# Weight pieces put off only beside attentions, and the modulation units spread thinner over two mixers

## The reference

```
# block 1, two layers: i = 0 is mixer A (grouped-query attention), i = 1 is mixer B (neighbourhood attention)
mod_x = silu(c) @ w_mod[i] + b_mod[i];  mod_c = silu(c_ctx) @ w_mod[i] + b_mod[i]
sh, sc, g = split(mod, 3)                                # shift, scale, gain, 1024 each
hx = rms_norm(x, norm_g[i]) * (1 + sc_x) + sh_x          # the same for the context, hc
yx, yc = mixer(hx, hc, ...)                              # q, k, v, z = h @ w_in; (attention * silu(z)) @ w_out
x = x + g_x * yx;  ctx = ctx + g_c * yc                  # the context only after layer 0
# block 2, one layer
p = _rmsnorm(x) @ w_in_2                                 # m_q, m_k, ..., n_q, ..., n_z, g_a, g_b
ya = sigmoid(m_o) * layernorm(mlstm(silu(conv(m_q)), silu(conv(m_k)), m_v, ...)) * silu(m_z)
yb = nsa(n_q, ...) * silu(n_z)                           # three attentions: compressed, selected, window
merged = sigmoid(g_a) * (ya @ w_branch_a) + sigmoid(g_b) * (yb @ w_branch_b)
out = _rmsnorm(x + merged @ w_out)
```

## Time and profile before

| | |
|---|---|
| three runs | 1679.43, 1682.07, 1684.57 us |
| profiled execution, its own time | 1678.06 us |
| its span | 1676.3 us |
| mean granted clock of PE over the span | 0.969 |
| PE busy | 1570.1 us, 94% |
| DVE, POOL, ACT busy | 725.5, 655.0, 621.6 us |
| weight loads by SP | 98 of 1024 KB |

### The profile page before, as it was taken

One profiled execution on the slowest core, in us unless ns is written; L12 is line 12 of the kernel. 1 busy time (PEld: TensorE's weight loads), 2 busy tenths in 40 slices (PEclk: granted clock), 3 DMA queues, 4 the chain that ended last, 5 costly groups with the idle time before them and its releaser, 6 DMA issues.

```text
span 1676.3 us, 25013 instructions
## 1 busy us (share of the span) xinstructions
PE 1570.1 (94%) x9858; PEld 1225.3 (73%) x9858; DVE 725.5 (43%) x1707; ACT 621.6 (37%) x1301; POOL 655.0 (39%) x640
## 2 busy tenths in 40 slices
PE   5998999999899899999999889999999899998987
PEld 3776777666688788787967677887877765555755
DVE  4334444444542524544465453452415444554023
ACT  4244443434542433334344343443332433332221
POOL 2534443334442533434344353534436243333242
PEclk8999999999999899999999899999999999999998
DMA  9111202221013222222221222212221212111121
GB/s 388 51 51 51 73 29 76 76 76 52 26 55 122 101 70 81 77 76 83 76 70 51 82 79 73 83 69 76 75 76 51 101 51 76 51 51 33 69 85 66
DMA packets 22148, 128.20 MB, mean 76 GB/s; under 512 B 2448, under 2 KB 2576, under 8 KB 8080
## 3 DMA queue, kind: packets, MB, share of 16 engines
q1 hardware_dynamic: 21888, 126.35, 20.8%
q10 hardware_dynamic: 144, 0.26, 0.1%
HBM read 124.50 MB, written 2.10 MB: 76 GB/s over the span
## 4 chain that ended last, share of the span: by engine, by line
PE 80%; DVE 8%; ACT 3%; issue 3%; POOL 3%; DMA 2%; SPq 0%; POOLq 0%; DVEq 0%; ACTq 0%
PE PS L1405 15%; PE PS L1407 14%; PE PS L1406 14%; PE PS L1485 6%; PE PS L1495 6%; PE PS L1520 6%; PE PS L1651 3%; PE PS L1400 2%; PE PS L1401 2%; PE PS L1402 2%; DVE sm L2099 2%; PE PS L1661 2%; POOL WL L2420 2%; DMA W<-in_wu 1%; PE PS L1573 1%
## 5 line engine op out<-in xcount | busy, mean ns | idle before, releaser
L2420 POOL TENSOR_TENSOR WL<-W,WH 128x512 fp32r<-128x512 f32 x280 | 365.2, 1321 | 330.4 <-ACT WH L1681 330.3
L1405 PE MATMUL PS<-HX,WH 128*128 128x512 f32 x1008 | 424.4, 421 | 33.3 <-POOL WL L2420 15.7
L1407 PE MATMUL PS<-HX,WL 128*128 128x512 f32 x1008 | 403.3, 400 | 0.0
L1406 PE MATMUL PS<-LX,WH 128*128 128x512 f32 x1008 | 402.6, 399 | 0.0
L1405 PEld LDWEIGHTS PS<-HX,WH 128*128 128x128 f32 x1008 | 195.3, 194 | 84.3 <-issue 32.2
L1407 PEld LDWEIGHTS PS<-HX,WL 128*128 128x128 f32 x1008 | 194.7, 193 | 43.6
L1406 PEld LDWEIGHTS PS<-LX,WH 128*128 128x128 f32 x1008 | 195.6, 194 | 38.1 <-issue 3.4
L1681 ACT CAST WH<-W 128x512 fp32r<-128x512 f32 x296 | 170.8, 616 | 26.6 <-PE PS L1402 18.5
L1767 ACT ACTIVATE AR<-PS,sm 128x768 f32<-128x768 f32 (+4 forms) x160 | 115.7, 723 | 170.6 <-DVE sm L2104 103.7
L2099 DVE TENSOR_REDUCE sm<-PS 128x1 f32<-128x512 f32 (+4 forms) x224 | 150.1, 670 | 57.8 <-PE PS L1485 53.0
L2487 POOL TENSOR_SCALAR AR<-AR,sm 128x768 f32<-128x768 f32 (+1 forms) x96 | 76.2, 793 | 210.4 <-DVE sm L2115 210.2
(11 more groups left out here) (273 smaller groups left out, 2464.5 us busy)
## 6 DMA issues: line engine op xcount, KB each, us to landing
W<-in_wu SPq DMA_DIRECT2D x98, 1024.0 KB, 4.8
AR<-in_wu SPq DMA_DIRECT2D x8, 1024.0 KB, 11.6
AR<-in_biasb SPq DMA_DIRECT2D x32, 256.0 KB, 2.6
XX<-in_xt SPq DMA_DIRECT2D x2, 1024.0 KB, 6.0
out<-XX SPq DMA_DIRECT2D x8, 256.0 KB, 2.2
XC<-in_xt SPq DMA_DIRECT2D x1, 1024.0 KB, 14.3
C<-in_cc SPq DMA_DIRECT2D x1, 770.5 KB, 8.4
CS<-in_cs SPq DMA_DIRECT2D x1, 512.0 KB, 9.9
```

Of the source, the lines that this page charges most:

```text
L1405: e.matmul(o, wh, xh, start=(k == 0), stop=False)
L1406: e.matmul(o, wh, xl, start=False, stop=False)
L1407: t = e.matmul(o, wl, xh, start=False, stop=(k == 7))
L2420: e.tensor_tensor(WL[:, d, a:z], W[:, n % 2, a:z], WH[:, d, a:z].bitcast(F32), ALU.subtract).then_inc(*s_wl_pool.by(n, q))
```

## The change

It has four parts. Pieces are put off by the rule of 9 only while `attention()` runs (`careful`); elsewhere each tick puts one in. In mixer A each pair from 1 to 7 has one modulation unit, in the first half of its queries, and pair 7 a second one in the last half of its gates; `aout` has four, as before, and the last four of the list go into the second half of each `bz` unit of mixer B. The `gain` steps of layer 1 stand behind `aout`, not ahead of it. In the `wa` units the ticks stand at k = 3 and k = 7 of each half.

```diff
--- before.py
+++ after.py
@@ unit_order
     for i in range(1, 8):
-        u += [("aqz", i)] + (m[2 * i - 2:2 * i] if i < 7 else [])
+        u += [("aqz", i), m[i - 1]]
+    u += [m[7]]
     for i in range(4):
-        u += [("aout", i), m[12 + i]]
+        u += [("aout", i), m[8 + i]]
     for a in range(4):
-        u += [("bz", a - 2)] if a >= 2 else []
+        u += [("bz", a - 2), m[10 + a]] if a >= 2 else []
         u += [("bqk", 2 * a), ("bqk", 2 * a + 1), ("bv", a)]
-    u += [("bz", 2), ("bz", 3)]
+    u += [("bz", 2), m[14], ("bz", 3), m[15]]
@@ tick
-            if pieces and (forced or done_work[0] - loaded_at[pieces[0][0]] > 9):
+            if pieces and (forced or not careful[0] or done_work[0] - loaded_at[pieces[0][0]] > 9):
@@ attention
             spent = [0.0]
+            careful[0] = True
...
             run(fill)
+            careful[0] = False
@@ mixer A
-        units_, riding = iter(MA[:12]), [iter(())]
+        units_, riding = iter(MA[:8]), [iter(())]
...
-                yield from query_group(pair, 0, FX, {1: ride_mm, 5: ride_tr})
+                yield from query_group(pair, 0, FX, {2: ride_mm, 6: ride_tr})
...
-                yield from gate_group(pair, 1, FC, {5: ride_mm_x})
+                yield from gate_group(pair, 1, FC, {3: ride_mm_x, 6: ride_tr} if pair == 7 else {})
                 yield PAUSE
-                ride_tr()
@@ out_proj
-                        run(mod_)
+                        next(mod_, None)
@@ mixer A to B
-        for k in range(0, KC, 2):
-            do("gain", 1, k)
-        out_proj("aout", 0, FULL, False, "o", ["b"], MA[12:])
+        out_proj("aout", 0, FULL, False, "o", ["b"], MA[8:12])
         ar = Arena()
         hb1 = Rows(ar(4096), ar(2048))
+        for k in range(0, KC, 2):
+            do("gain", 1, k)
@@ gen_z
-                yield from pj(("bz", m), un, 0, T, 128 * (m % 2), "b", o)
+                for k in range(8):
+                    yield from pj(("bz", m), un, 0, T, 128 * (m % 2), "b", o, (k,))
+                    if m % 2 and k == 2:
+                        mod_ = mod_units(*MA[12 + a][:1], MA[12 + a][1:], pr)
+                        next(mod_)
+                    if m % 2 and k == 6:
+                        next(mod_)
@@ the wa units
                 for m in range(2):
-                    tick()
                     wps["wa", j, m] = (un.n, bank(FC.take(("wa", j, m), (s_mg, (j, m)))))
                     for k in range(8):
+                        if k % 4 == 3:
+                            tick()
                         do("x_wa", j, m, k)
```

More of the change, by code:

```diff
@@ L294, in build @@
         COST = {"proj": 0.6, "score": 1.0, "turn": 0.5, "pv": 0.7, "x_wa": 0.9, "mod_mm": 0.9, "m_qk": 0.9, "m_num": 1.0}
-        done_work, loaded_at = [0.0], {}
+        done_work, loaded_at, careful = [0.0], {}, [False]
         def do(*item):
@@ L881, in build @@
         norm("b", Arena(6144), X_CTX, [(s_post, ("a", 47))], lambda k, p: [(s_res, ("aout", k, p))])
+        out_proj("aout", 0, FULL, False, "o", ["b"], MA[8:12])
+        ar = Arena()
+        hb1 = Rows(ar(4096), ar(2048))
         for k in range(0, KC, 2):
             do("gain", 1, k)
-        out_proj("aout", 0, FULL, False, "o", ["b"], MA[12:])
-        ar = Arena()
-        hb1 = Rows(ar(4096), ar(2048))
         for part in range(2):
```

## The result

| | before | after |
|---|---|---|
| runs, median | 1682.39 us (4 runs, 1679.43 to 1684.57) | 1642.43 us (4 runs, 1640.18 to 1646.11) |
| profiled execution, its own time | 1678.06 us | 1641.75 us |
| span | 1676.3 us | 1640.0 us |
| mean granted clock | 0.969 | 0.978 |

The ratio is 0.9766, with a 95% interval from 0.9742 to 0.979: 40.0 us less, where 29 were forecast.

The account below looks back on a forecast made before the run. PE, busy 94% of the span, bounds the kernel, so only its idle or slow places can gain. 23.8 + 12.3 − 6.3 − 0.5 = 29.3 us less gives 1653 us in runs, forecast 1648 to 1657, range 1641 to 1668.

Parts of the forecast that it names:

- the clock: Slow stretches behind waits that go: 1.7 us each in mixer A and gb 1, 2.4 at wo 0, some in nz 1.
- The fourth rival: The change does more: no slow stretches in mixer A, nz 1's whole wait, half the mod_mm time; 1643 us, chance 0.17.
- The pieces outside attentions: Block 2 to its end: earlier casts and subtractions remove PE's waits for POOL's low parts of weights, 23.8 us gained.
- nz 1: First two of six casts move ahead of the compressed attention's last exponential, the last stay: 2.0 us of at most 5.6.
- Mixer A: Fewer modulation units: waits for DVE's last step and for a load go, 5.9 us each; 12.3 us gained in sum.
- I take one of the three as gained: Mixer A: of three slow stretches beside waits, 5.1 us in all, one goes, 1.7 gained; 3.4 left out.
- Pair 7: End of mixer A: two units added, the first costing 1.6 us, the second 2.6 with a bank wait of 1.8.
- Mixer B: PE is busy throughout, so four added modulation units at 1.58 us each are paid in full: 6.3 us lost.
- the third rival: Each mixer B unit waits a whole landing for its load, costing 43.2 us in place of 6.3: 1690 us, chance 0.03.
- the first rival: The attentions give nothing, since exponentials set mixer A's pace; only the stages outside gain: 1659 us, chance 0.15.
- The gains: Eight small DVE instructions now between output projection and next norm, where PE waits for DVE: about 0.5 us lost.
- The second rival: Early pieces hold ACT or stretch DVE's two-input work by 1.0 us each, losing half of 23.8: 1665 us, chance 0.12.

Follow-up runs that it names:

- rule_only: The kernel before with only the rule for pieces (put off beside attentions only) and the changed wa ticks, modulation units as before: 1654.80 us, ratio 0.9871.
- turn_inside: The kernel before with one edit, the mod_tr of the gates' unit at the gates' last step, not behind them: 1680.25 us, ratio 1.001.
- units_only: The changed kernel with the old rule for pieces and old wa ticks, modulation units and gains as in the change: 1670.02 us, ratio 0.9961.
- the change, second group: The changed kernel, unedited, run again on a second chip for comparison, against the kernel before: 1643.60 us, ratio 0.9794.
- the change, third group: The changed kernel, unedited, run again on a third chip for comparison, against the kernel before: 1645.74 us, ratio 0.9819.
- nz_late: The changed kernel with the pieces used by nz 1's second half put off as before: 1649.84 us, ratio 0.9842.
- wa_ticks_old: The changed kernel with the ticks in the wa units once per half as before: 1645.19 us, ratio 0.9821.

## Why the prediction was right, and what was mis-sized

The direction, the range (1641 to 1668) and the waits that go were right; the likeliest time, 1653, was 10.6 us too high. The term that was mis-sized is the clock. The fourth rival, at 1643, came nearest, by its slow stretches that stay away, and that is partly luck: it depends on the execution.

- **The pieces outside attentions: 23.8 forecast.** Between the gates of block 2 and the last norm the traces of the change show 36.3 − 11.2 = 25.1 us, and the run with the rule alone 23.0. mk 0 to nz 0 gave 18.5 − 11.2 = 7.3 (forecast 4.7 + 1.1 + 1.4 = 7.2). gb 1 to wo 1 gave 36.4 − 22.9 = 13.5 (forecast 14.6). The pieces of wo 1 still had no wait, so the 0.3 us for the queue were not needed. This stage is the firmest of all: from ga 0 to the last norm the three kernels with late pieces take 308.6 to 308.9 us, and the eleven traces with early ones 295.4 each.
- **nz 1: 2.0 forecast,** 4.4 in the traces of the change, 2.6 in rule_only's with the same pieces. The last pieces didn't move, as forecast, and the idle time fell by 1.4. The rest is clock: in the three profiled executions of the changed kernel no slow stretch stood there, in five other kernels with these pieces early one or two did. So 2.0 was not far off, and the 4.4 are partly luck.
- **Mixer A: 12.3 forecast, 15.0 measured** (score 44; 15.5 and 14.3 in the two other executions). That all 11.8 us of the two waits go was right, though I had added them as if each stood for itself: in turn_inside, where only one of them goes, nothing is gained. That the mod_mm out of the gates give nothing was right too: the waits for the exponentials grew by 6.3 us. The boundaries to pairs 2 and 3 gave 0.0 by score 19, where I had 1.0; but a slow stretch at 158 us is twice as long there as before, and from first score to score 19 the two other executions gained 1.3 and 1.7. From score 19 to 25 and from 25 to 31 it was 4.5 us each, to 37 it was 6.0. The too small term is "I take one of the three as gained": by windows of 4 us from 108 us to mixer A's end slow stretches cost 7.1 us before, and 2.9, 2.8 and 4.8 in the three executions of the change. In the first none stood behind 166 us; in the others one and two came in pair 7. Pair 7: +2.6 and −2.7, forecast −2.6 for its second unit.
- **Mixer B: −6.3 forecast,** −5.9 in the change, −6.7 and −6.6 in its other executions, −6.7 with the units alone. It is busy throughout, and no unit waited for its load: the third rival had no part. Nor had the first rival, that the exponentials eat the gain.
- **The gains: −0.5 forecast.** From score 44 to mixer B's first step it went 0.6 the other way in this trace, and −0.3 and −0.9 in the two other executions, with slow stretches in all of them. A price of this size can't be told from the clock.
- **The second rival,** that pieces beside DVE's work cost what they save: the price is there, and no wait of PE grew by it. In the changed kernel's compressed attention, before and beside POOL's pieces:

```profile
1313.21 0.43 DVE L2384 TENSOR_TENSOR AR<-AR,C 128x256 f32<-128x256 f32 x1
...
1321.12 1.46 DVE L2384 TENSOR_TENSOR AR<-AR,C 128x256 f32<-128x256 f32 x1
```

The same factor as in the earlier trace rows; PE's next wait on DVE there is 0.8 us in both kernels. The Trainium skill, "GPSIMD Engine Reference", section "1. Specifications", has GpSimd's ways into SBUF shared with VectorE, as the prediction said. This trace agrees again (0.43 against 1.46), and it decided nothing.

- **The clock.** Over windows of 4 us between 100 and 1628 us, (1 − clock) × busy time sums to 30.9 us before and 16.1 after: 14.8 of the 36.3 us. The forecast had 1.7 + 1.7 + 2.4 and a part of nz 1, some 6.5. This is the one term that was too small: I took each slow stretch only where it stood behind a large wait that goes. What is left is idle time, less the modulation units that are now paid in full, and there the forecast held:

| trace | ahead at the last norm | of it clock | the rest |
|---|---|---|---|
| forecast | 29.3 | 6.5 | 22.8 |
| the change | 36.3 | 14.8 | 21.5 |
| the change, second group | 33.8 | 12.0 | 21.8 |
| the change, third group | 31.0 | 9.3 | 21.7 |
| rule_only | 20.7 | 3.8 | 16.9 |
| units_only | 8.8 | 4.9 | 3.9 |

The rest is the same within 0.3 us in all three executions, and the two parts add up to it within 1 us. The last stage, from ga 0 on, has slow stretches in all three kernels with late pieces (4.0 to 4.3 us) and in none of the eleven traces with early ones: there the clock went with the waits.
- **From the profile to the runs.** I carried 4.0 us from the profiled execution to the median. After the change this distance is 0.7. That is 3.3 us of the miss. On other chips the kernel before has medians of 1675 to 1679 and the changed one of 1643.6 and 1645.7; the first chip's comparison shows the largest gain of the three.

What stays open: why the gain is 40.0, 35.4 and 29.4 us on three chips. The clock has a part. In the three profiled executions it is all of the difference, and where 29.4 us were gained the kernel before had the faster clock (median 0.971 over its runs, against 0.967 where it was 35.4; the changed kernel had 0.972 to 0.978 and 0.972 to 0.979). What makes a slow stretch come or go wasn't tried.

## What to carry to other kernels

Put a task where the engine waits for something else anyway, right before that wait, and check that the waiting step is really the next one: the same unit cost about 0.7 us there (an estimate: 1.6 less the 0.9 that a pair got shorter), 1.5 to 1.7 in a stage without slack, and 2.1 at another step of the pair. When two waits stand in a row, removing the first may only lengthen the second; count what is late next before adding them. An order that bunches small conversions behind a chain of another task can cost more than its idle time: from ga 0 on 13.4 us were won, where the waits had been 6.0 + 4.8 = 10.8. Compare traces with the clock taken out, since the traces of one kernel lay 5.3 us apart by slow stretches alone.

## What was not expected of the hardware

Slow stretches (the clock at 1.2 in place of 2.4 GHz) stood behind some waits, and none behind the waits of 1.5 and 0.9 us in nz 1 in the three profiled executions of the changed kernel. In nz_late the clock was at 0.57 from 1312 on, before the wait of 3.90, in a window where PE was busy throughout, and in wa_ticks_old, whose code is the changed kernel's up to there, at 0.57 from 1310 on. In the kernel before it fell at 1111.5 us though PE had been busy without a gap:

```profile
1108.00:1111.50 3.50, 3.50 (x27) 0.99 0.01 2
1111.50:1115.00 3.50, 3.50 (x10) 0.52 0.87 302
```

So they are not only a matter of the wait just passed. Executions of one program on one chip differed by 10 us of 1680, with the mean clock between 0.963 and 0.973.
